# Moving the norm weight into the activation tiles, all low parts of the up weights to VectorE, and the two table-free products of steps 0 and 1 to the front

## The reference, cut to what matters

```python
D_MODEL = 1024; SEQ = 1024; D_FF = 4096
def rmsnorm(x, w):
    return x * lax.rsqrt(jnp.mean(jnp.square(x), axis=-1, keepdims=True) + EPS) * w
# one layer, float32
mix = hybrid_mixer(rmsnorm(h, norm_in), ...)      # latent attention + state space, w_out
h   = h + rmsnorm(mix, norm_post)
hm  = rmsnorm(h, norm_mlp)                        # norm_mlp: "the norm weight" below
f   = jnp.square(jax.nn.relu(hm @ w_mlp_up))      # 1024 x 1024 times 1024 x 4096
h   = h + rmsnorm(f @ w_mlp_down, norm_mlp_post)
```

## Time and profile before

| | |
|---|---|
| median of three runs | 1576.49 us (1573.24 to 1577.84) |
| the profiled execution | 1577.22 us, span 1575.4 us |
| mean granted TensorE clock | 0.99 |
| busy TensorE, VectorE, GpSimd, ScalarE | 98%, 67%, 54%, 43% |
| first up banks, steps, down products (last stage) | up to 965 us, 967 to 1252 us, from 1255 us |

### The profile page before, as it was taken

How to read it: one execution, slowest core, us unless ns; L and a number is a source line. 1 busy time by engine, 2 the same in 40 slices (tenths; PEclk the granted TensorE clock), 3 DMA queues, 4 the chain that set the end, 5 groups by cost and what they waited for, 6 DMA issues and landing times.

```text
span 1575.4 us, 22595 instructions
## 1 busy us (share of the span) xinstructions
PE 1537.2 (98%) x7951; PEld 1319.7 (84%) x7951; DVE 1061.1 (67%) x1617; ACT 684.6 (43%) x1329; POOL 849.1 (54%) x746
## 2 busy tenths in 40 slices
PE   8999999999999999999999997999999999999997
PEld 8999998878888888788887886788888788888885
DVE  4856516256766767677778779866666567747776
ACT  5322212144544444566664452444444445444542
POOL 7534444155777646943321428888888224405553
PEclk9999999999999999999999998999999999999999
DMA  6454622236555455699978641444444597636666
GB/s 214 113 144 122 171 54 67 67 89 178 158 169 168 138 152 170 228 334 322 327 274 294 253 128 56 141 146 154 152 154 154 201 349 242 203 104 197 188 199 147
DMA packets 225795, 280.63 MB, mean 178 GB/s; under 512 B 21401, under 2 KB 148225, under 8 KB 225697
## 3 DMA queue, kind: packets, MB, share of 16 engines
q1 hardware_dynamic: 224688, 275.69, 54.0%
q0 software_dynamic: 1008, 3.67, 1.3%
HBM read 180.63 MB, written 98.66 MB: 177 GB/s over the span
## 4 chain that ended last, share of the span: by engine, by line
PE 84%; POOL 5%; DVE 5%; DMA 2%; issue 1%; ACT 1%; SPq 1%; DVEq 0%; POOLq 0%; ACTq 0%
PE ps L2960 19%; PE ps L2951 13%; PE ps L825 7%; PE ps L884 6%; PE ps L2899 4%; PE ps L2823 4%; PE ps L1799 4%; PE ps L1785 2%; PE ps L1768 2%; PE ps L840 2%; PE ps L856 2%; PE ps L1716 2%; PE ps L1738 2%; PE ps L458 1%; PE ps L2928 1%
## 5 line engine op out<-in xcount | busy, mean ns | idle before, releaser
L2960 PE MATMUL ps<-dw_hi,df_hi 128*128 128x512 f32 x448 | 176.5, 394 | 5.4 <-DVE dw_lo L3632 5.4
L2960 PE MATMUL ps<-dw_lo,df_hi 128*128 128x512 f32 x448 | 176.0, 393 | 0.0
L2960 PE MATMUL ps<-dw_hi,df_lo 128*128 128x512 f32 x448 | 175.7, 392 | 0.0
L178 POOL TENSOR_TENSOR ring<-stage,zero 128x512 fp32r<-128x512 f32 (+2 forms) x75 | 83.6, 1115 | 152.2 <-DMA stage<-w_in 48.8
L3627 DVE TENSOR_TENSOR df_lo<-df_raw,df_hi 128x512 fp32r<-128x512 f32 x112 | 121.7, 1086 | 47.6 <-ACT df_hi L3267 47.3
L2960 PEld LDWEIGHTS ps<-dw_hi,df_hi 128*128 128x128 f32 x448 | 85.1, 190 | 23.9 <-issue 6.2
L3632 DVE TENSOR_TENSOR dw_lo<-dw_raw,dw_hi 128x512 fp32r<-128x512 f32 x96 | 80.7, 840 | 35.6 <-ACT dw_hi L3276 23.8
L3267 ACT ACTIVATE df_hi<-df_raw 128x512 fp32r<-128x512 f32 x112 | 70.3, 627 | 77.5 <-DMA df_raw<-d_f 77.0
L180 POOL TENSOR_TENSOR ring<-stage,ring 128x512 fp32r<-128x512 f32 (+2 forms) x75 | 100.5, 1340 | 5.9
L2960 PEld LDWEIGHTS ps<-dw_hi,df_lo 128*128 128x128 f32 x448 | 85.2, 190 | 18.0
L2960 PEld LDWEIGHTS ps<-dw_lo,df_hi 128*128 128x128 f32 x448 | 85.2, 190 | 17.7
(11 more groups left out here) (542 smaller groups left out, 4557.7 us busy)
## 6 DMA issues: line engine op xcount, KB each, us to landing
df_raw<-d_f SPq DMA_DIRECT2D x112, 256.0 KB, 2.7
d_f<-fa SPq DMA_DIRECT2D x105, 256.0 KB, 2.1
dw_raw<-w_mlp_down SPq DMA_DIRECT2D x96, 256.0 KB, 3.0
landA<-w_mlp_up SPq DMA_DIRECT2D x52, 256.0 KB, 3.9
stage<-w_in SPq DMA_DIRECT2D x40, 256.0 KB, 2.7
stage<-w_out SPq DMA_DIRECT2D x28, 256.0 KB, 4.2
xt<-x SPq DMA_DIRECT2D x8, 512.0 KB, 7.7
d_xT<-xdT SPq DMA_DIRECT2D x8, 512.0 KB, 3.3
```

The lines of the kernel that those rows point to most:

```text
L178: pool.tensor_tensor(hi, src, k.zero[:, 0:1].broadcast_to([P, width]), ALU.add).then_inc(k.sem(fam + "_hi"), 1)
L2960: mm = pe.matmul(ps[:, base + t, :], F_AT[q % SLOTS][a][:, P * t:P * t + P], W_AT[q % SLOTS][b][:, :], start=(fresh and (a, b) == (0, 0)), ...
```

## The change

1. The norm weight is applied where tiles are cut, by one pointer scale per 128x128 block (ScalarE and VectorE), and no longer to any weight.
2. GpSimd keeps the four sums of a step, and VectorE cuts all seven lows: five ahead of the two totals, two behind them.
3. TensorE's order in steps 0 and 1 becomes the list FLOW, with A11 and A12 of both steps first.
4. ScalarE makes the highs of step 0 between tiles 6 and 7, and those of A11 and A12 of step 1 right behind tile 7.
5. Loads of step 0 are issued before the last store; all four loads of step i+2 wait for the sums of step i+1 and its lows of A11, A12 and A22.
6. The first two cuts of the down stage move ahead of step 13's last relu and square.

```diff
+    FLOW = [(0, "A11"), (0, "A12"), (1, "A11"), (1, "A12")] + [(0, q) for q in ("S1", "S2", "S4", "S3", "A22")]
+    FLOW += [(1, q) for q in ("S1", "S2", "S4", "S3")] + [(2, "A11"), (1, "A22")] + [(2, q) for q in PRODUCTS[1:]]
+    FLOW += [(i, q) for i in range(3, STEPS) for q in PRODUCTS]
...
+            if t == LAST:
+                sp.wait_ge(sem("v_cut"), HALF - EARLY)
+                load_quarter(0, "A11")
+                load_quarter(0, "A22")
+                sp.wait_ge(sem("m_mm"), len(UNITS))
+                load_quarter(0, "A21")
+                load_quarter(0, "A12")
             store_h(t)
...
             if i + 2 < STEPS:
-                sp.wait_ge(sem("x_plo"), 4 * (i + 1) + 1)
-                load_quarter(i + 2, "A21")
-                load_quarter(i + 2, "A11")
-                sp.wait_ge(sem("x_dlo"), 3 * (i + 1) + 3)
-                load_quarter(i + 2, "A22")
-                load_quarter(i + 2, "A12")
+                sp.wait_ge(sem("x_raw"), 4 * (i + 1) + 4)
+                sp.wait_ge(sem("x_dlo"), max(low_made(i + 1, q)[1] for q in ("A11", "A12", "A22")))
+                for q in ("A21", "A11", "A22", "A12"):
+                    load_quarter(i + 2, q)
...
+            pool.tensor_tensor(s1, a21, a22, ALU.add).then_inc(own, 1)
+            pool.wait_ge(own, 4 * i + 1)
+            pool.tensor_tensor(s2, s1, a11, ALU.subtract).then_inc(own, 1)
+            pool.tensor_tensor(s3, a11, a21, ALU.subtract).then_inc(own, 1)
...
+            pool.tensor_tensor(s4, a12, s2, ALU.subtract).then_inc(own, 1)
...
-            if q == "A11":
-                pe.wait_ge(sem("v_sq"), (6, 8)[i] if i < 2 else UP + 4 * (i - 1))
+            if i < 2 and q in ("A11", "S1", "A12"):
+                pe.wait_ge(sem("v_sq"), {"A11": (3, 7), "S1": (4, 8), "A12": (5, 7)}[q][i])
+            elif q == "A11":
+                pe.wait_ge(sem("v_sq"), UP + 4 * (i - 1))
...
-                act.activation(HM[0][:, 4 * c:4 * c + 4, P * t:P * t + P], ps[:, TURN_BANKS[t % 2][c], :].rearrange("p (a b) -> p a b", b=P),
-                               ACT.Copy).then_inc(sem("m_hi"), 1)
+                for j in range(4):
+                    mm = act.activation(HM[0][:, 4 * c + j, P * t:P * t + P], ps[:, TURN_BANKS[t % 2][c], P * j:P * j + P], ACT.Copy,
+                                        scale=col(k, "mlp", 4 * c + j))
+                mm.then_inc(sem("m_hi"), 1)
...
+                for j in range(4):
+                    hi, lo = (x[:, 4 * c + j, P * t:P * t + P] for x in HM)
+                    mm = dve.scalar_tensor_tensor(lo, ps[:, TURN_BANKS[t % 2][c], P * j:P * j + P], col(k, "mlp", 4 * c + j), hi.bitcast(F32),
+                                                  ALU.mult, ALU.subtract)
+                mm.then_inc(sem("m_lo"), 1)
...
-            if more:
-                weight_low(i + 1, "A22")
-                weight_low(i + 1, "S3")
-                weight_low(i + 1, "A12")
+            for q in lows[:5]:
+                weight_low(i + 1, q)
             total(i, 0)
             total(i, 1)
+            for q in lows[5:]:
+                weight_low(i + 1, q)
```

More of the change, by code:

```diff
@@ L2291, in phase_rest, with sub_end, highs, dlows @@
     RESULTS = (("A21", Y, 2), ("A22", V, 1), ("A11", Z, 0), ("A12", X, None))
[L2292 to L2295, removed]
+    FLOW = [(0, "A11"), (0, "A12"), (1, "A11"), (1, "A12")] + [(0, q) for q in ("S1", "S2", "S4", "S3", "A22")]
+    FLOW += [(1, q) for q in ("S1", "S2", "S4", "S3")] + [(2, "A11"), (1, "A22")] + [(2, q) for q in PRODUCTS[1:]]
+    FLOW += [(i, q) for i in range(3, STEPS) for q in PRODUCTS]
+    at_product = {x: UP + n + 1 for n, x in enumerate(FLOW)}
+    def sub_end(i):
+        return at_product[i, "A22"]
+    def highs(i):
+        return ("A11", "A12", "A22", "S1", "S2", "S3", "S4") if i == 1 else ("A22", "S1", "A11", "S2", "S3", "A12", "S4")
+    def dlows(i):
+        return highs(i)
+    def low_made(i, q):
+        return "x_dlo", 7 * i + dlows(i).index(q) + 1
     def unsplit(i, q):
@@ L2648, in weights_begun @@
                 pool.wait_ge(sem("x_q0"), 64)
[L2649 to L2668, removed]
+                pool.wait_ge(sem("m_weighted"), len(FUSED))
@@ L2677, in weights_ended @@
[L2677 to L2680, removed]
+            if i >= 2:
+                pool.wait_ge(sem("v_up"), sub_end(i - 2))
+            s1, s2, s3, s4 = (sums[i % 2][q][:, :, :] for q in ("S1", "S2", "S3", "S4"))
+            a11, a12, a21, a22 = (unsplit(i, q)[:, :, :] for q in ("A11", "A12", "A21", "A22"))
@@ L3017, in on_tensor @@
             up_bank(n)
-        for i in range(STEPS):
-            for n in range(7):
-                product(i, n)
+        for i, q in FLOW:
+            product(i, q)
         down_products()
@@ L3227, in on_scalar @@
         high_tile(NT - 2)
+        weights_high(0, "S2", "S3", "A12", "S4")
         first_relu(2)
         high_tile(NT - 1)
[L3230 to L3233, removed]
+        weights_high(1, "A11", "A12")
+        for n in range(3, 7):
             first_relu(n)
-        act.wait_ge(sem("x_tstep"), 16)
         act.wait_ge(sem("m_mm"), len(UNITS) + 1)
@@ L3250, in on_scalar @@
             if more:
-                weights_high(i + 1, "A22", "S1", "A11")
+                weights_high(i + 1, *(("A22",) if i == 0 else ("A22", "S1", "A11")))
             if i:
                 kept(i, 1)
-            if more:
+            if i == 0:
+                weights_high(1, "S1", "S2", "S3", "S4")
+            elif more:
                 weights_high(i + 1, "S2", "S3")
@@ L3257, in on_scalar @@
                 kept(i, 2)
[L3258 removed]
+            if more and i:
                 weights_high(i + 1, "A12", "S4")
[L3260 removed]
+            for n in range(3):
                 relu(i, n)
[L3263 to L3276 removed]
+            if not more:
+                act.wait_ge(sem("fresh"), 2)
+                down_high(0)
+                down_high(1)
+            relu(i, 3)
         def keep(p, bank, dst):
@@ L3538, in up_sub @@
             summed_tile(i, 2)
+            if not more:
+                dve.wait_ge(sem("fresh"), 2)
+                down_low(0)
+                down_low(1)
             squared(i, 3)
@@ L3603, in on_vector @@
         table_step(2)
-        for q in ("A22", "S3", "A12"):
+        for q in dlows(0):
             weight_low(0, q)
@@ L3610, in on_vector @@
         first_square(5)
+        weight_low(1, "A11")
+        weight_low(1, "A12")
         table_step(6)
```

134 lines of the change are left out of this document (62 added, 72 removed).

## The result

The changed kernel takes 1581.24 us (median of seven runs, 1580.79 to 1584.54), the kernel before 1574.40 in the same comparison (1571.24 to 1577.84). The ratio is 1.0045, with a 95% interval of 1.0031 to 1.0059: slower by 6.8 us by the medians, where +6.0 was forecast. The absolute forecast of 1582.5 us stood on 1576.5 for the kernel before, which took 1574.4 here, so of the two only the difference bears on the prediction's sum.

What follows compares the result with a forecast made beforehand. TensorE, busy 98% of the span, was taken as the bound, with only waits, gaps and low clock to win. Terms -2.1 (up to (0,A22)), +9.5 (steps behind), -1.4 (down products) gave +6.0 on 1576.5: 1582.5 us, range 1569.5 to 1592.

Steps and rivals of the forecast that it cites:

- Tile 7: Before the steps: tile 7's norm ends at 939.1, its last low at 949.6; the banks end at 973.4, +8.2 us.
- The price of 1.05 us for a sum: VectorE beside GpSimd: the two take turns, so each GpSimd sum costs VectorE about 1.0 to 1.1 us, taken as 1.05.
- the 0.28 taken for VectorE's small cut: Tile cuts: a 128x128 pointer cut on VectorE takes 0.28 us, from the row for a 128x128 subtraction.
- The two old waits: Ahead of step 0's S1: TensorE's waits of 1.9 and 6.7 us both go, covered by four table-free products of 10.9 us.
- (0,A22): Last product of step 0: reached at 995.3, a new 5.5 us wait until 1000.8; -2.1 us against before.
- Steps behind: After (0,A22): clock and late kept copies, 0.5 us in each of ten late steps; 12.6 us against 3.1, +9.5.
- Down products: Start of the down products: two VectorE instructions leave the path of the 3.45 us wait, -1.4 us.
- loads in time: Rival, late steps: GpSimd starts within 5 us of first load issue, kept copies never late; 1573.6 us; chance 0.17.
- The sums miss: Rival at tile 7: step 0's sums miss its norm, as loads land after 932; -4.2, 1578.3 us; chance 0.13.
- Hardly stop each other: Rival, VectorE beside GpSimd: at 0.4 us a sum, no wait at (0,A22) and no late-step waits; 1567.7 us; chance 0.10.
- The rival with the clock: Rival, late steps: each of the ten waits also costs 1.6 us of clock; +16, 1598.5 us; chance 0.07.

Runs made afterwards that it cites:

- run 3: Changed kernel with ScalarE making the seven highs of step 0 behind tile 7's cut, as before the change: 1577.82 us, 1.0019 of before.
- run 6: run 3 with GpSimd's four sums of step 0 starting only when tile 7's norm is done: 1574.53 us, 0.9996 of before.
- run 7: Changed kernel with the 128x512 cuts back in all hm tiles and the norm weight left out altogether: 1576.27 us, 1.0006 of before.
- run 5: Changed kernel with TensorE's order alone put back, all seven products step by step: 1580.45 us, 1.0039 of before.
- run 1: Changed kernel with ScalarE's kept copy of S1 ahead of the next step's high of A11, from step 1 on: 1572.4 us, 0.9981 of before.
- run 2: Changed kernel with VectorE cutting the low of A12 ahead of the two totals, from step 1 on: 1571.02 us, 0.9973 of before.
- run 4: Changed kernel with step 0's two totals ahead of the five lows of step 1 on VectorE: 1580.73 us, 1.0038 of before.
- run 8: Changed kernel with the edits of run 1, run 2, run 3 and run 4 together: 1564.88 us, 0.9937 of before.
- run 10: run 8 with TensorE's order of before the change: 1567.63 us, 0.9954 of before.

## Why the prediction was right

**Tile 7** was to end its norm at 939.1 and its last low at 949.6; it did so at 938.3 and 948.7 (946.54+2.16). The banks were to end 8.2 us late and ended 7.2 late: the path was the one put down. Runs 3, 6 and 7 show each of the three causes by itself: the highs ahead (3.8 us at up_bank(4)), the turn-taking with the sums (4.3 on the norm, run 6 against run 3), the small cuts (1.1 on the norm, 3.5 on the last low). The price of 1.05 us for a sum fits: four of them, 4.2 put down. So does the 0.28 taken for VectorE's small cut, for which no row had the form: eight took 2.16 us, 0.27 each.

**The two old waits** went, for the reason given; run 5 brings the larger back with 4.78.

**(0,A22)** was to start at 1000.8 behind 5.5 us; it started at 999.96 behind 5.60. Against before that is -3.0 where -2.1 was put down (999.96-5.46-997.47).

**Steps behind**: +9.5 put down, +10.5 measured. From the start of (0,A22) to the end of the last product it takes 259.3 us (999.96 to 1259.30); before, it takes 254.3 with two products more to do, so 5.46 are taken off, 248.8. Against 90 products at 2.73 (245.7) the changed kernel loses 13.6 us, where 12.6 were put down. By place, from the starts of the products: 1.5 by the clock at (0,A22) (1.7 put down), 1.0 at (1,S4) (1.35), 3.2 at (2,S4) (2.85) and 1.7 by the clock behind it (1.7), and 6.3 from step 3 on (5.0). A late step takes 19.77 us, above the 19.5 to 19.7 foreseen, and 0.66 more than the ideal 19.11, not 0.5. The waits listed there are 0.20 to 0.51; the list counts them from the end of the last matmul, and a matmul of 0.39 us ends 0.16 later than the next one could have started (one pitch of 0.23). With 0.08 more in the first matmul behind each wait (0.47 long) that makes the 0.66. Runs 1 and 2 show the chain at two of its links.

**Down products**: -1.4 put down; TensorE's gap, the last pitch off, fell from 3.6 to 2.3 us, -1.3.

**The sum** to the start of the down products is +6.2 in the traces (1255.34 to 1261.58) and +6.8 in the medians; +6.0 was forecast.

Of the rivals, "loads in time" falls: the sums began 2.5 to 3.2 us into a late step (one step began at 1101.82, its first sum at 1104.48), and from the first issue to the first sum 6.7 us went by (1078.24 to 1084.90; the chain above shows the issues from the second on). The estimate from the Trainium skill (DMA: Bandwidth & Descriptors, Anatomy of one DMA — SWDGE (gpsimd) path) was 4.4; its formula is for one DMA issued by GpSimd, and here SyncE issues four. "The sums miss" falls with the first sum at 927.65 (928 put down). "Hardly stop each other" falls with 4.55 for the table step. The rival with the clock falls too, as the matmuls behind the waits of 0.20 to 0.51 are not slow: they last 0.47 and then 0.39 to 0.40 us, not 0.63.

What the prediction didn't see is how the terms hang together. It added the gain of the new order and the losses of steps 1 and 2 as separate terms; run 5 shows that the losses are the gain handed back, and that the order by itself is worth nothing that can be measured here. The sum came out right since both were in it.

## What to carry to other kernels

Before unloading an engine, look for a wait that names it. Here none named GpSimd; it gave up 148 us for nothing, and the price of its moved work was a longer loop through VectorE and SyncE. For every load ask which instruction sets it free and follow the loop once around: if it is as long as the step, each queue on it must hold nothing else ahead. And a wait that is taken away shows what it covered, so runs of single edits can win nothing (4) where the edits together win 16 us (8).

## What was not expected of the hardware

GpSimd's first sum at 966.27 took 4.55 us against 1.29 alone, while VectorE ran two lows and a table step (966.11 to 969.66) at their undisturbed 1.28 and 2.35 us: the two don't always take turns one for one. Nor do all of VectorE's instructions pay. In run 6 four sums ran from 933.87 to 939.02 beside VectorE's first squares and a tile's low cut, which read one operand from PSUM, and all went at their undisturbed 1.28 to 1.29 (sum), 1.29 (two squares) and 2.16 us (eight cuts). The price of 1.05 us for a sum was met beside instructions whose two operands both lie in SBUF.

The 2.7 us by which the two profiled executions differ in the down products are clock. Behind the first wait, the slow matmuls ended 6.3 us after its end before (1255.34 to 1261.59) and 4.2 after it now (1261.58 to 1265.76), for waits of 3.45 and 2.12 us; the stretch up to the last wait is 1.1 us longer before. Behind that last wait, of nearly the same length, the matmuls were slow only before (granted clock 0.50 from 1548.0 to 1551.4; after the change 1.00 from 1553.1 to 1556.5), and the rest of the span is 1.5 us longer. The kernel before, then the changed one:

```profile
1547.95 0.75 PE L2960 MATMUL ps<-dw_hi,df_hi 128*128 128x512 f32 x1 [1.96 <-DVE dw_lo L3632]
1548.50 0.63 PE L2960 MATMUL ps<-dw_lo,df_hi 128*128 128x512 f32 x1
```

```profile
1553.08 0.47 PE L2954 MATMUL ps<-dw_hi,df_hi 128*128 128x512 f32 x1 [2.00 <-DVE dw_lo L3542]
```

The same wait does not always cost the same. At the start of the down products the changed kernel and all eleven runs wait 2.1 us; slow matmuls follow in five of the twelve traces (the changed kernel, runs 1, 4, 6 and 10) and none in the other seven. In the changed kernel eleven matmuls took 4.2 us there instead of 2.5. So two single traces can differ by some 1.7 us with no cause that the record shows, and a forecast that adds 1.7 us of clock behind a wait of 2 us has a term that comes or does not. Behind the waits of 3.05 us and more inside the steps slow matmuls followed in every trace.
